# A merged hybrid block with interleaved tracks: order of the first loads, joint Ln/Exp tables, modulation chunks in pairs, and side steps moved behind modulation steps

## What is computed

```
xbc = silu(causal_depthwise_conv(xbc)); dt = softplus(dt_raw + dt_bias)
y   = ssd_chunked_scan(x, dt, a, B, C) + x * d_skip
yg  = y * silu(z); yg = yg * rsqrt(mean(yg*yg) + eps)        # per group
h   = h + (g0 * (attn @ w_a) + g1 * (ssm @ w_s)) @ w_out
h   = h + swiglu(rmsnorm(h)); x = rmsnorm(h)
```

```
mx = split(silu(c) @ w_mod[l] + b_mod[l], 9)                 # layer l, 9 x 1024 columns
x  = x + 0.5 * mx[2] * swiglu(rmsnorm(x) * (1 + mx[1]) + mx[0])
```

## Time and profile before

| what | value |
|---|---|
| median of three runs | 2839.81 us |
| the profiled execution | 2841.48 us |
| its span, first to last instruction | 2839.7 us |
| TensorE busy | 2596.8 us, 91% |
| VectorE busy | 1378.9 us, 49% |
| ScalarE busy | 1044.0 us, 37% |
| DMA | 372.36 MB, mean 131 GB/s |
| mean granted TensorE clock | 0.954 |

### The profile page before, as it was taken

The page is one execution under the profiler, slowest core; times in us unless marked ns, Lnnn a source line. Parts: engine busy times, 40 slices in busy tenths (PEclk is TensorE's granted clock), DMA queues, the critical chain, the costliest instruction groups (busy, mean ns, idle before and its releaser), DMA issues. The chain is left out here.

```text
span 2839.7 us, 36318 instructions
## 1 busy us (share of the span) xinstructions
PE 2596.8 (91%) x15294; PEld 2159.7 (76%) x15294; DVE 1378.9 (49%) x2279; ACT 1044.0 (37%) x1628; POOL 0.2 (0%) x4
## 2 busy tenths in 40 slices
PE   5999899899989999989888999989999896758999
PEld 5887679878867888867666888868888784446898
DVE  3746454554444333367865333343333354556654
ACT  3534454433333222245542222132222243344443
POOL 0000000000000000000000000000000000000000
PEclk8999999999999999989989999999999997769999
DMA  6886643488842222335002322322222243021454
GB/s 229 273 253 207 207 134 111 134 303 301 295 155 83 98 98 98 97 117 167 1 23 75 98 98 98 98 76 96 97 96 97 89 150 94 1 74 39 160 182 140
DMA packets 145188, 372.36 MB, mean 131 GB/s; under 512 B 20202, under 2 KB 65794, under 8 KB 144898
## 3 DMA queue, kind: packets, MB, share of 16 engines
q1 hardware_dynamic: 144402, 367.82, 40.2%
q10 hardware_dynamic: 624, 2.21, 0.2%
HBM read 368.84 MB, written 1.15 MB: 130 GB/s over the span
## 5 line engine op out<-in xcount | busy, mean ns | idle before, releaser
L298 DVE TENSOR_TENSOR weights_lo<-weights_raw,weights_hi 128x1024 fp32r<-128x1024 f32 (+1 forms) x545 | 656.1, 1216 | 536.0 <-ACT weights_hi L292 533.8
L344 PE MATMUL psum<-normed_hi,weights_hi 128*128 128x256 f32 (+1 forms) x2560 | 866.8, 339 | 38.5 <-DVE normed_lo L543 28.1
L344 PE MATMUL psum<-normed_lo,weights_hi 128*128 128x256 f32 (+1 forms) x2560 | 847.3, 331 | 0.0
L344 PE MATMUL psum<-normed_hi,weights_lo 128*128 128x256 f32 (+1 forms) x2560 | 846.7, 331 | 0.0
L292 ACT CAST weights_hi<-weights_raw 128x1024 fp32r<-128x1024 f32 (+1 forms) x545 | 562.0, 1039 | 382.3 <-DMA weights_raw<-in_w_down 267.3
L344 PEld LDWEIGHTS psum<-normed_hi,weights_hi 128*128 128x128 f32 x2560 | 488.7, 191 | 136.5 <-issue 67.3
L344 PEld LDWEIGHTS psum<-normed_lo,weights_hi 128*128 128x128 f32 x2560 | 490.0, 191 | 43.7 <-issue 1.2
L344 PEld LDWEIGHTS psum<-normed_hi,weights_lo 128*128 128x128 f32 x2560 | 489.4, 191 | 44.4
L344 PE MATMUL psum<-hidden_hi,weights_hi 128*128 128x512 f32 x528 | 205.4, 389 | 0.0
L344 PE MATMUL psum<-hidden_lo,weights_hi 128*128 128x512 f32 x528 | 205.4, 389 | 0.0
L344 PE MATMUL psum<-hidden_hi,weights_lo 128*128 128x512 f32 x528 | 205.4, 389 | 0.0
(11 more groups left out here) (290 smaller groups left out, 2886.5 us busy)
## 6 DMA issues: line engine op xcount, KB each, us to landing
weights_raw<-in_w_gu SPq DMA_DIRECT2D x220, 512.0 KB, 3.5
weights_raw<-in_w_down SPq DMA_DIRECT2D x110, 512.0 KB, 3.5
arena<-in_w_mod SPq DMA_DIRECT2D x72, 512.0 KB, 5.5
resid<-in_w_mod SPq DMA_DIRECT2D x24, 512.0 KB, 5.2
normed_raw<-in_w_mod SPq DMA_DIRECT2D x24, 512.0 KB, 5.5
under_normed_hi<-in_w_mod SPq DMA_DIRECT2D x24, 512.0 KB, 5.3
weights_raw<-in_w_x SPq DMA_DIRECT2D x24, 512.0 KB, 4.5
weights_raw<-in_w_qk SPq DMA_DIRECT2D x24, 512.0 KB, 3.8
```

The costliest lines, as they stand in the source:

```text
L298: ve.tensor_tensor(w_lo[:, c % RING, a], w_raw[:, c % RING, a], w_hi[:, c % RING, a].bitcast(F32), ALU.subtract).then_inc(lo_ready, 1)
L344: last = te.matmul(out, a, b, start=start and n == 0, stop=stop and n == 2)
```

## The change

- `Setup`: SyncE waits for x and for the constants and rows before it issues the first three weight chunks; the tables of the relative bias and the bias move from ScalarE's queue to SyncE's, behind these chunks.
- `Norm`, `DtChain` and `Gating` load table set 6 explicitly in place of the one-column Ln, or ahead of their Ln and Exp.
- `Modulation` takes two chunks in a step: a round has a turning step and four chunk steps, 46 steps in all in place of 82. Loads and waits are per chunk as before.
- `woven`: the steps of the third track are placed at the next place of the second track, and so stand directly behind that modulation step. The third segment lists Modulation second and LoadContext third.

```diff
 def woven(tracks):
-    steps = []
+    steps, second = [], []
     for n, (stages, a, b) in enumerate(tracks):
         mine = [(stage, i) for stage in stages for i in range(stage.n)]
-        steps += [(a + (b - a) * (j + 0.5) / len(mine), n, j, *step) for j, step in enumerate(mine)]
+        places = [a + (b - a) * (j + 0.5) / len(mine) for j in range(len(mine))]
+        if n == 1:
+            second = places
+        if n == 2:
+            places = [min([p for p in second if p >= place], default=place) for place in places]
+        steps += [(place, n, j, *step) for j, (place, step) in enumerate(zip(places, mine))]
     return [(stage, i) for _, _, _, stage, i in sorted(steps, key=lambda s: s[:3])]
...
+        def load_tables():
+            se.add_instruction(mybir.InstLoadActFuncSet(name=nc.get_next_instruction_name(),
+                                                        act_func_set_id=TABLES_LN_EXP, ins=[], outs=[]))
...
 class Norm(Stage):
...
             def scalar(self, act, step, i):
...
-                se.activation(small[:, 703:704], ones[:, 0:1], ACT.Ln)
+                load_tables()
                 act.wait_ge(norm_vv, self.vv0 + 1)
...
         class Setup(Stage):
...
             def sync(self, sp, i):
                 sp.dma_start(resid[:, :, TOK], W["x"]).then_inc(tokens_in, 16)
+                sp.wait_ge(tokens_in, 16)
+                sp.wait_ge(const_in, 32)
                 for c in range(LEAD):
                     load_chunk(sp, c)
+                sp.dma_start(rel_tables.rearrange("p a n -> p (a n)"),
+                             consts[:, where["onehot"][0]:where["onehot"][0] + 2 * TOEP]).then_inc(rel_in, 16)
+                sp.dma_start(small[0:N_BUCKETS, 0:NG * HG], W["rel_bias"]).then_inc(rel_in, 16)
...
-                act.dma_start(rel_tables.rearrange("p a n -> p (a n)"), consts[:, kept:kept + 2 * TOEP]
-                              ).then_inc(rel_in, 16)
-                act.dma_start(small[0:N_BUCKETS, 0:NG * HG], W["rel_bias"]).then_inc(rel_in, 16)
...
         class Modulation(Stage):
...
-                self.n = MOD_ROUNDS * (KD + 1) + 1
+                self.n = MOD_ROUNDS * (KD // 2 + 1) + 1
...
-                r, k = divmod(i, KD + 1)
-                return self.first + r, k - 1
+                r, k = divmod(i, KD // 2 + 1)
+                return self.first + r, 2 * k - 2
...
-                    self.load(sp, (r - self.first) * KD + k + MOD_RING)
+                    for m in range(2):
+                        self.load(sp, (r - self.first) * KD + k + m + MOD_RING)
...
-                    pe.wait_ge(mod_landed[c % MOD_RING], 16 * (c // MOD_RING + 1))
                     if k == 0 and r > self.first:
                         pe.wait_ge(mod_read, r)
-                    for g in range(4):
-                        last = te.matmul(psum[32 * g:32 * g + 32, MOD_BANK, 0:MOD_W], cond[:, k, :],
-                                         self.ring[c % MOD_RING][:, g, :],
-                                         start=k == 0, stop=k == KD - 1, tile_position=(0, 32 * g))
-                    last.then_inc(mod_used, 1)
+                    self.chunk(pe, r, k)
+                    self.chunk(pe, r, k + 1)
+
+            def chunk(self, pe, r, k):
+                c = r * KD + k
+                pe.wait_ge(mod_landed[c % MOD_RING], 16 * (c // MOD_RING + 1))
+                for g in range(4):
+                    last = te.matmul(psum[32 * g:32 * g + 32, MOD_BANK, 0:MOD_W], cond[:, k, :],
+                                     self.ring[c % MOD_RING][:, g, :],
+                                     start=k == 0, stop=k == KD - 1, tile_position=(0, 32 * g))
+                last.then_inc(mod_used, 1)
 
             def scalar(self, act, step, i):
                 r, k = self.at(i)
-                if k == KD - 1:
+                if k == KD - 2:
                     act.wait_ge(mod_used, KD * (r + 1))
...
         class DtChain(Stage):
...
                 if i == 0:
+                    load_tables()
                     step(se.activation(a_exp, row("a_log"), ACT.Exp))
...
         class Gating(Stage):
...
                 if i == SG:
+                    load_tables()
                     for half in range(2):
...
         segments.append(([
             ([attn_branch, mixer_out, norm2, *ffn0, last_norm], 0, 1),
+            ([Modulation(1, mod_ring1, (a1_max, NT * HG))], 0.1, 0.95),
             ([LoadContext()], 0.1, 0.2),
-            ([Modulation(1, mod_ring1, (a1_max, NT * HG))], 0.1, 0.95),
```

More of the change, by code:

```diff
@@ L301, in build @@
         bank_free = []
+        TABLES_LN_EXP = 6
+        def load_tables():
+            se.add_instruction(mybir.InstLoadActFuncSet(name=nc.get_next_instruction_name(),
+                                                        act_func_set_id=TABLES_LN_EXP, ins=[], outs=[]))
         class Stream(Stage):
@@ L695, in sync @@
                 if k >= 0:
-                    self.load(sp, (r - self.first) * KD + k + MOD_RING)
+                    for m in range(2):
+                        self.load(sp, (r - self.first) * KD + k + m + MOD_RING)
             def tensor(self, pe, i):
                 r, k = self.at(i)
-                c = r * KD + k
                 if i == 0:
@@ L1572, in build @@
         TURN_BANK = 7
-        TABLES_LN_EXP = 6
-        def load_tables():
-            se.add_instruction(mybir.InstLoadActFuncSet(name=nc.get_next_instruction_name(),
-                                                        act_func_set_id=TABLES_LN_EXP, ins=[], outs=[]))
         def steps_of(*stages):
```

## The result

| | before | after |
|---|---|---|
| median | 2839.30 us (4 runs, 2838.00 to 2842.81) | 2803.84 us (4 runs, 2802.40 to 2808.34) |
| ratio | | 0.9870 (0.9858 to 0.9883) |
| the profiled execution | 2841.48 us | 2803.61 us |
| its span | 2839.7 us | 2801.8 us |
| mean granted clock | 0.954 | 0.956 |

A forecast was written before the change was run, and what follows sets the result against it. TensorE, busy 91% of the span, was taken as the bound. Terms -12.6 - 9.0 - 18.9 + 0.4 + 2.5 = -37.6 took the profiled 2841.5 to 2803.9, so a median of 2802 us, range 2790 to 2816.

The forecast's parts named there:

- The start: Kernel start up to the first product: x lands at about 10.6, first product at 24.8; gain 12.6 us.
- The tables: Norms: seven more table loads of 1.28 us leave the wait for the Exp; gain 9.0 us, norm1's counted in the start.
- The visits: Modulation chunks in pairs, first and third segments: 11.3 and 7.6 us, gain 18.9 less 0.4.
- The waits: TensorE's waits: scans 3.6, gating 3.5 and 1.1, seam to the second segment 6.9; 15.1 us in sum.
- The slow clock behind the waits: Slow matmuls after waits: some 3 us before, perhaps 2 now; with the waits' +3.5 a cost of 2.5 us.
- part is eaten by the DMAs: Rival: DMA limits in the first segment and at the start take part of the gain; 2807 to 2818, chance 0.17.
- The loads don't do what they say: Rival: Ln and Exp still get table loads of their own, 10 us of gain go; 2812, chance 0.03.
- a hidden drain: Rival: a drain no row shows goes with each load, VectorE's wait shrinks by 2.66; 2791, chance 0.02.
- The clock falls in the scans and the gating: Rival: idle TensorE drops to its lower clock from the first pair to the seam; 2897, chance 0.04.
- The seam and the clock do better: Rival: clock stays high through the first product, or the seam costs 3 us less; 2787 to 2795, chance 0.12.

The follow-up runs named there:

- e4: The kernel before with only the pairs, two modulation chunks per step: 2815.27 us, ratio 0.9910.
- e2: The kernel before with only the edit of Setup, the new order of the first loads: 2840.78 us, ratio 1.0000.
- e3: The kernel before with only the explicit table loads: 2829.38 us, ratio 0.9957.
- e1: The changed kernel without the rule that puts side steps behind modulation steps: 2791.67 us, ratio 0.9831.
- e5: The kernel before with only the rule for side steps, 82 modulation steps and the old track order: 2848.86 us, ratio 1.0028.
- e11: The kernel before with the rule for side steps and the third segment's tracks in the changed order: 2841.02 us, ratio 1.0005.
- e6: The changed kernel with the rule lifted for the load of the relative tables and the gating steps: 2796.09 us, ratio 0.9839.
- e12: The changed kernel without the rule, with modulation visits of four chunks and gating sums one step later: 2778.41 us, ratio 0.9786.
- e8: The changed kernel without the rule, with the third segment's first six modulation chunks asked for earlier: 2787.27 us, ratio 0.9812.
- e7: The changed kernel without the rule, with modulation visits of four chunks in place of two: 2780.80 us, ratio 0.9785.

## Why the prediction was right

2802 was forecast and 2803.84 measured; 2803.9 was the sum for the profiled execution, and 2803.61 it took. The mechanisms named were there, and the waits came out one by one. That the sum is right to 0.3 us is luck: up to norm2 the lead is some 7 us less than the sum's terms say, and that was made up for behind the second block's first Ln, as the points show.

- **The start**, 12.6 predicted, 11.6 measured. x at 10.6, measured 10.77; the first product at 24.8, measured 25.82. The chain of norm1 took 15.05 in place of 14.2; in it the 16 sums of squares took 6.38 for 5.67 before. e4 and e2 give the cause of the gain: the shift of the first modulation step, not the edits of `Setup`.
- **The tables**, 7 x 1.28 and one in the start, 10.2 in all, with DtChain's 0.9. Each norm's Exp stands directly behind its Ln. The two head norms of the last layer, 2.6 us, were missing from the sum. e3 gave 10.7, whose interval (8.5 to 16 us) has room for both sums. The Trainium skill (ScalarE: Activation LUTs, What ACT_TABLE_LOAD costs) counts about 2.66 us for a switch with its drain. The trace does not agree: eight of them would be 21 us.
- **The visits.** 0.19 for coming and going and 0.43 for the second chunk held, and for four chunks as well. Third segment: 7.6 predicted for the pairs; from norm2 to the last norm's Ln it took 248.6 before and 238.9 after, 9.7, of which 1.28 is a table load, so 8.4.
- **The waits.** Scans 3.6 predicted, 3.5 measured, four of 0.5 and one of 1.6 as forecast; gating 3.5 and 1.1, measured 3.6 and 1.1; seam 6.9, measured 2.48 + 3.70 = 6.2, for a low part first and then for the bank. Together 14.4 for 15.1.
- **The slow clock behind the waits was priced too low.** From the first product to the attention the sum had 11.3 - 0.4 - 2.5 = 8.4; measured were 17.5 - 11.6 = 5.9, although the waits were 0.7 shorter. The sum let the slow matmuls behind the waits fall from 3 us to 2. But in the four windows at 0.50 shown above TensorE works for 12.9 us, and in the two of the kernel before for 7.2. At half speed I estimate that as 2.8 more, in place of 1 less.
- **What was missing:** from the attention to norm2 the changed kernel loses 17.5 - 14.1 = 3.4 us that no term of the sum held. Its first pair waits 3.9 in all for its chunks, 1.7 more than before, and the granted clock of the stretch is 0.96 in place of 0.99. e1 has the same wait (4.0) at a clock of 0.98 and takes 161.7 there, 2.4 less than the changed kernel, so the greater part goes with the clock of that execution.
- **What made up for it:** behind the second block's first Ln, where only table loads were changed, the changed kernel gains 37.9 - 24.2 = 13.7. Five loads of norms and two of head norms at 1.28 are 9.0; the sum had 6.4. The other 4.7 go with the clock of that execution, as far as can be told (below).
- **A step that was priced right but judged too mildly:** the sum booked the new waits against the old ones, +3.5, and with the clock 2.5, and so showed the rule as small. Against the kernel with pairs and without the rule (e1) it costs 12.2 us, a third as much as the whole change gains. The pairs alone had already brought the gating from 10.7 to 6.6, so most of the old waits were not there to be won by the rule. Of the swap of tracks the prediction said that it only puts the context load behind a modulation step; e5 and e11 show that, with the rule and 82 steps, it saves 8 us.

Of the rivals, *part is eaten by the DMAs* is refuted: between 40 and 130 us TensorE waits for no chunk. *The loads don't do what they say* is refuted by the trace, *a hidden drain* by e3. *The clock falls in the scans and the gating* came true in small, in short stretches behind the waits. *The seam and the clock do better* did not happen in the changed kernel; e1, without the rule, is in its range.

## What to carry to other kernels

Price a reordering against the version that has all the other edits, not against the kernel before: here a rule that costs 12 us sat inside a change that gains 36, and a list sorted from fractions moved steps (x at the start, the modulation in e5) that the edit never named. Where a small foreign matmul interrupts a dense stream, the price is per visit, so make the visits fewer and longer as long as the ring supplies them. When two versions differ by less than the clock makes the same work vary, compare the start of a common instruction ahead of the stages where it varies.

## What the runs showed of the hardware

**The same work takes 1981 or 1991 us, and the granted clock goes with it.** Behind the second block's first Ln the changed kernel, e1 and e6 run the same instructions. Windows of that part (rounded to whole us), of the changed kernel, of e6 and of e1:

```profile
820.00:2801.00 1981.00, 1809.95 (x9074) 1491.34 (x9074) 949.41 (x1597) 677.89 (x1092) 0.00 (x0) 0.95 0.29 95
```

```profile
813.00:2794.00 1981.00, 1809.28 (x9074) 1492.28 (x9074) 949.38 (x1597) 678.56 (x1092) 0.00 (x0) 0.95 0.29 95
```

```profile
806.00:2797.00 1991.00, 1823.23 (x9074) 1500.70 (x9074) 949.52 (x1597) 678.61 (x1092) 0.00 (x0) 0.94 0.29 94
```

9074 matmuls in all three, VectorE and ScalarE equally busy, and TensorE busy 13 us longer in e1. It shows in the attention mixer of the last layer, from the Ln of its norm to that of the next. The changed kernel, then e1:

```profile
2235.30:2597.21 361.91, 271.72 (x1398) 207.01 (x1398) 200.77 (x418) 140.07 (x253) 0.00 (x0) 0.84 0.25 74
```

```profile
2220.19:2592.95 372.76, 285.84 (x1398) 216.57 (x1398) 200.77 (x418) 140.40 (x254) 0.00 (x0) 0.81 0.24 72
```

It is a matter of the execution, not of the kernel: e12 took 2773.0 at a mean granted clock of 0.958, and 2786.9 at 0.950. What decides it in an execution stays open.

**The longer waits cost more than themselves.** In the changed kernel the waits of 1.6, 3.6, 2.48 and 3.70 us each stand at a stretch of 3.4 us with a granted clock of 0.50 or 0.51. Behind the gating wait of 1.1 it stayed at 1.00 (324.9 to 328.3), and so it did behind e1's wait of 1.2 at the seam (359.3 to 362.7). Where a wait of 4.0 went, e8 gained 5.7 us up to norm2, and e7, which has visits of four as well, 5.1.

**A table load costs its own 1.28 us and no more here:** the two head norms' waits shrank from 23.04 to 21.75 and from 27.34 to 26.04 when the Exp's load went from the chain ahead of each.
